# Three-pass weight tiles between the heads of an attention loop, gate writes in eighths, and four value buffers at the end of an expert sweep

## The chip, the cores and the metric

The kernel runs on one core of one Trainium2 chip. The metric is the device time of one execution in microseconds; less is better. TensorE's granted clock has two levels here, 1.2 and 2.4 GHz; a clock of 1.00 in a row is 2.4 GHz throughout the stretch.

## What is computed

One layer of a hybrid block on 512 tokens of width 1024, in float32, ending in a norm. Cut to what matters:

```python
mod = silu(c) @ w_ada + b_ada            # shift1, scale1, gate1, shift2, scale2, gate2
h = modulate(rmsnorm(x), shift1, scale1)
proj = h @ w_in                          # qa ka va | qb kb vb | ga gb
ya = swa_sink_attention(rope(qa), rope(ka), va, sinks) @ w_up_swa   # 8 heads, 2 of keys, window 128
yb = stick_breaking_attention(qb, kb, vb) @ w_up_sb                 # 8 heads, strictly causal
x = x + gate1 * ((sigmoid(ga) * ya + sigmoid(gb) * yb) @ w_out)
h2 = modulate(rmsnorm(x), shift2, scale2)
# PEER: product keys pick 16 of 16384 experts for each of 8 heads and token
x = x + gate2 * sum_k gelu(h2 . expert_u[k]) * g[k] * expert_v[k]
out = rmsnorm(x)
```

## The kernel before

The kernel is one program with an order written out by hand for each engine; semaphores join them. SP (SyncE) issues nearly all loads, in one order, and a wait on it holds up all loads behind it. An engine's buffers lie in one arena, and areas are used again from stage to stage.

**Start.** Six parts of `mod` come from twelve 2 MB tiles of `w_ada`, through a ring of four slots: VectorE multiplies a tile with `silu(c)` (`ada_product`, 8 steps) and TensorE sums over the partitions (`ada_sum`, four f32 products of one column); the third tile goes through TensorE directly. Then `h` is normed and modulated (ScalarE L839). VectorE works out the rope angles behind that (L1132 to L1142).

**Head loop** (about 53 to 439 us). Four pairs of heads. Each turn loads `w_pair` (2 MB, from GpSimd's queue) and makes the projections qa, qb, kb (L584) and vb (L588) in plain f32 from `h`. VectorE makes two ada products, then rope. For each of the two heads follow sliding-window scores (L606 to L613, the head's 64 rows), stick-breaking scores in four blocks of 512 to 128 columns in four PSUM banks (L619), one gate block of 512 tokens, in f32 (L625, kept in `early_gates`), the turned probabilities (L632), the sums of the logarithms (L638 to L643), and the two outputs of 64 columns (L649, L655). Beside it ScalarE takes absolute values, exponentials and logarithms, VectorE maxima, scalings and copies out of PSUM.

**Up and out** (439 to 581 us). `UNITS` lists 24 weight tiles of 128x1024: 8 ups, the 8 gate blocks of m = 4 to 7 between them, and 8 outs. Each is split into a high part (ScalarE `unit_high` L893) and a low part (VectorE `unit_low` L1198), two tiles deep, and TensorE makes three passes (`PASSES`: high x high, low x high, high x low) in float32r, so 24 products of 512 columns a tile (L691). The first ups use the gates that were kept. After the last up all of `merged` is split (L910, L1202; seven of the eight low parts come ahead of the last merge).

**Ranking** (594 to 873 us). Queries, top-k and the first 36 chunks (`EARLY`) of `expert_u`: `scores(c)` is 24 products of 384 columns (L729). The 384 tokens of three tiles take all experts in chunks of 128 (there are 128 chunks); the fourth tile's tokens take their 128 picked experts by gathers (`gather` L506), with VectorE's `dot` (L1243) and `add_row` (L1350).

**Gates** (873 to 1124 us). 36 chunks (`BESIDE`) of scores with 96 groups of one-hot products (L773) between them. After each 16 groups a stage buffer of 4 MB is full, and SP writes it to memory with two transfers of 2 MB in runs of 256 bytes (L429), between the loads of `expert_u` (`u_load` L406). Scores before `STASHED` are passed through gelu and put into memory too.

**Values.** Four more chunks of scores, then 52 (`NF`) steps of one `scores` and one `values(i)` (18 products of 512 columns, L785), to 1595 us, then 76 steps of `values` alone, to 1939 us. Weights are gelu x gate (VectorE `weights` L1395), split by ScalarE (L1066) and VectorE (L1400) into one of two `ar` buffers; value rows are split by ScalarE (L1051) and VectorE (L1383) into one of two `vs` buffers. Each engine does one chunk and waits for the next one. `dots_before` and `accs_before` say how many dots and added rows lie between. At the end the last chunk finishes all six banks, tile by tile, and VectorE and ScalarE do gate2, sum, norm and output of four token tiles (L1422 to L1431).

## Time and profile before

| | us |
|---|---|
| median of 3 runs (1956.57 to 1959.97) | 1956.68 |
| profiled execution | 1958.36 |
| its span, first to last instruction | 1956.4 |

| engine | busy us | share |
|---|---|---|
| TensorE products | 1815.1 | 93% |
| TensorE weight loads | 1500.4 | 77% |
| VectorE | 1325.8 | 68% |
| ScalarE | 693.5 | 35% |
| GpSimd | 535.2 | 27% |

The chain of work that ended last is TensorE for 74% of the span, VectorE 10%, DMA 5%, ScalarE 5%. TensorE's weight loads (PEld) overlap its products (PE). In the rows below, the view of windows gives for each stretch its length and, for PE, PEld, DVE (VectorE), ACT (ScalarE) and POOL (GpSimd), busy us and the number of instructions, then the granted clock, the share of the DMA engines and GB/s. In a timeline a row is a group of like instructions in a row: start, length, and in brackets the idle time before it with what ended it. An f32 product is recorded as two instructions, a three-pass one as one for each pass. L12 is line 12 of the kernel.

### The profile page before, as it was taken

What the parts mean: (1) busy time and instruction counts of PE and PEld (TensorE: products, weight loads), DVE (VectorE), ACT (ScalarE), POOL (GpSimd) and SP (SyncE); (2) the same over time, 40 slices, a digit from 0 to 9 for tenths busy, and PEclk for the clock granted to TensorE, in tenths of its full rate; (3) what the DMA queues carried; (4) which work ended last, traced back from release to release, by engine and by line L of the source; (5) the groups of instructions that cost most, each with busy time, mean ns of one, the idle gap of its engine ahead of it and who ended that gap; (6) DMA issues with size and microseconds to landing.
All of it is one profiled execution on the core that took longest, in us unless ns stands there. A gap on an engine that the chain in (4) does not pass through costs nothing.

```text
span 1956.4 us, 24506 instructions
## 1 busy us (share of the span) xinstructions
PE 1815.1 (93%) x8747; PEld 1500.4 (77%) x8747; DVE 1325.8 (68%) x2755; ACT 693.5 (35%) x1072; POOL 535.2 (27%) x326
## 2 busy tenths in 40 slices
PE   5899999989988999989989969999999999999996
PEld 4555555558867999979989959999999987777774
DVE  5423232335437699989788848888877888888886
ACT  2231415153326444334343323333333333333333
POOL 0000000000004576460000035545553443333330
PEclk7989798889998999989999989999999999999998
DMA  8414030202222434346888799999998989999992
GB/s 314 179 43 150 12 139 21 86 7 90 93 90 81 143 119 144 98 160 164 221 241 226 204 324 377 338 344 335 339 339 297 324 311 341 342 338 341 344 342 107
DMA packets 221696, 416.21 MB, mean 213 GB/s; under 512 B 112305, under 2 KB 148145, under 8 KB 217649
## 3 DMA queue, kind: packets, MB, share of 16 engines
q1 hardware_dynamic: 173232, 257.70, 39.3%
q0 software_dynamic: 37440, 142.62, 20.5%
...
## 4 chain that ended last, share of the span: by engine, by line
PE 74%; DVE 10%; DMA 5%; ACT 5%; issue 4%; SPq 2%; POOL 0%; DVEq 0%; ACTq 0%
PE bank L729 22%; PE bank L785 19%; PE bank L691 6%; PE bank L584 4%; PE bank L709 4%; DMA u_raw<-euT 4%; PE bank L625 3%; PE bank L773 2%; PE bank L619 2%; PE bank L588 1%; ACT v_split L1051 1%; DVE hot_j L1361 1%; PE bank L613 1%; DVE weights L1395 1%; DVE row_sum L1350 1%
## 5 line engine op out<-in xcount | busy, mean ns | idle before, releaser
L729 PE MATMUL bank<-h_split,u_split 128*128 128x384 f32 x3072 | 564.3, 340 | 18.3 <-DVE u_split L1339 15.7
L785 PE MATMUL bank<-v_split,a_split 128*128 128x512 f32 x2304 | 547.4, 393 | 21.8 <-DVE a_split L1400 20.0
L729 PEld LDWEIGHTS bank<-h_split,u_split 128*128 128x128 f32 x3072 | 541.0, 190 | 24.7 <-DVE u_split L1339 16.0
L785 PEld LDWEIGHTS bank<-v_split,a_split 128*128 128x128 f32 x2304 | 428.3, 188 | 127.6 <-issue 40.7
L506 POOL DMA_INDIRECT rows<-eu,idx x128 | 184.7, 1443 | 401.6 <-DVE dots L1243 376.7
L506 POOL DMA_INDIRECT rows<-ev,idx x128 | 180.4, 1410 | 269.7 <-DVE row_sum L1350 238.4
L1051 ACT ACTIVATE v_split<-v_raw 128x1024 fp32r<-128x1024 f32 x128 | 135.6, 1059 | 178.9 <-PE bank L785 174.9
L953 ACT ACTIVATE gelus<-bank 128x384 f32<-128x384 f32 x128 | 62.9, 491 | 352.7 <-PE bank L729 349.6
L1383 DVE TENSOR_TENSOR v_split<-v_raw,v_split 128x1024 fp32r<-128x1024 f32 x128 | 156.5, 1223 | 18.5 <-ACT v_split L1051 18.1
L1350 DVE SCALAR_TENSOR_TENSOR row_sum<-rows,agate,row_sum 128x1024 f32<-128x1024 f32 x127 | 162.6, 1280 | 4.3
L1339 DVE TENSOR_TENSOR u_split<-u_raw,u_split 128x1024 fp32r<-128x1024 f32 x90 | 109.9, 1221 | 74.3 <-ACT u_split L944 73.8
L944 ACT ACTIVATE u_split<-u_raw 128x1024 fp32r<-128x1024 f32 x128 | 134.5, 1052 | 56.6 <-DMA u_raw<-euT 56.6
L1243 DVE CUSTOM_DVE_ANT_0 rows<-rows,h_rows 128x1024 f32<-128x1024 f32 x128 | 150.6, 1220 | 1.7 <-issue 1.6
L1066 ACT ACTIVATE a_split<-weights 128x384 fp32r<-128x384 f32 x128 | 66.8, 522 | 173.0 <-DVE weights L1395 172.3
L483 POOL TENSOR_TENSOR query_lo<-query_raw,query_hi 128x2048 fp32r<-128x2048 f32 x8 | 37.3, 4663 | 322.0 <-ACT query_hi L937 322.0
L488 POOL TENSOR_TENSOR u_split<-u_raw,u_split 128x1024 fp32r<-128x1024 f32 x38 | 92.2, 2438 | 94.1 <-ACT u_split L944 94.1
L1395 DVE TENSOR_TENSOR weights<-gelus,gates 128x384 f32<-128x384 f32 x128 | 70.9, 554 | 57.9 <-issue 49.1
L773 PE MATMUL bank<-hot_i,hot_j 128*128 128x128 f32 x768 | 93.7, 276 | 14.3 <-ACT stage L1040 12.0
L1361 DVE TENSOR_SCALAR hot_j<-cst,slots_turned 128x128 f32<-128x128 f32 x384 | 106.3, 340 | 0.0
L1400 DVE TENSOR_TENSOR a_split<-weights,a_split 128x384 fp32r<-128x384 f32 x128 | 71.1, 555 | 51.9 <-ACT a_split L1066 51.9
L773 PEld LDWEIGHTS bank<-hot_i,hot_j 128*128 128x128 f32 x768 | 91.4, 192 | 15.6 <-issue 12.8
L709 PE MATMUL bank<-h_split,query_hi 128*128 128x512 f32 x256 | 81.9, 396 | 12.9 <-DVE h_split L1237 12.9
...
## 6 DMA issues: line engine op xcount, KB each, us to landing
u_raw<-euT SPq DMA_DIRECT2D x128, 512.0 KB
v_raw<-ev SPq DMA_DIRECT2D x128, 512.0 KB
arena<-w_ada SPq DMA_DIRECT2D x12, 2048.0 KB, 7.9
gates_scratch<-stage SPq DMA_DIRECT2D x12, 2048.0 KB, 19.6
gates<-gates_scratch SPq DMA_DIRECT2D x128, 192.0 KB
...
arena<-w_units SPq DMA_DIRECT2D x24, 512.0 KB, 3.5
```

Source lines behind the costliest of these rows:

```text
L506: pool.indirect_dma_start(rows[g % NG], None, eu if g < P else ev_rows, bass.IndirectOffsetOnAxis(ap=idx[:, g % P:g % P + 1], axis=0)).the ...
L691: last = pe.matmul(ps[bank][:], ws[:, t % 2, wp, k * P:(k + 1) * P], x_split[:, xp, k, :], start=(first and q == 0), stop=(end and q == 2))
L709: last = pe.matmul(ps[c][:], q_parts[n % 2][wp][:, k * 256 + c * P:k * 256 + (c + 1) * P], hs[:, xp, k, :], start=(k == 0 and q == 0), sto ...
L729: last = pe.matmul(ps[6 + b][:, 0:TD], us[:, b, wp, k * P:(k + 1) * P], hs[:, xp, k, 0:TD], start=(k == 0 and q == 0), stop=(k == DC - 1 a ...
L773: last = pe.matmul(ps[2 + b][:, q * P:(q + 1) * P], ohj[:, b, q, :], ohi[:, b, q, :], start=True, stop=True)
L785: last = pe.matmul(ps[2 * t + f][:], ar[:, b, ap, t * P:(t + 1) * P], vs[:, b, vp, f * 512:(f + 1) * 512], start=(first and q == 0), stop= ...
L944: act_(us[:, c % 2, 0, :], ut[:, c % RING, :], ACT.Copy).then_inc(u_hi, 1)
L1051: act_(vs[:, i % 2, 0, :], vt[:, i % RING, :], ACT.Copy).then_inc(v_hi, 1)
L1243: nv.tensor_tensor_reduce(rows[k % NG], rows[k % NG], hT, 1.0, 0.0, ALU.mult, ALU.add, dots[:, k:k + 1]).then_inc(rows_used, 1)
L1350: nv.scalar_tensor_tensor(acc, rows[g % NG], agate[:, k:k + 1], acc, ALU.mult, ALU.add).then_inc(rows_used, 1)
L1361: ins = nv.tensor_scalar(ohj[:, b, q, :], cst[:, K_IOTA:K_IOTA + P], slotsT[:, 1, t:t + 1], slotsT[:, 2, t:t + 1], ALU.is_equal, ALU.mult)
L1383: nv.tensor_tensor(vs[:, i % 2, 1, :], vt[:, i % RING, :], vs[:, i % 2, 0, :].bitcast(F32), ALU.subtract).then_inc(v_split, 1)
```

## The change

All 50 weight tiles of the attention and merge stages (18 projections, 16 gate blocks, 8 ups, 8 outs) now form one list `BLOCKS` and take one path: `block_load` on SP, four raw slots deep, `block_high` on ScalarE, `block_low` on GpSimd, two split buffers, three passes on TensorE. `h` is split into `h1s` at the start, by VectorE, chunk by chunk. Six blocks (`LEAD`) come before the first head; the others lie between the steps of the eight heads (`FILL`: two after the scores, the others after the sums), all 16 gates among them. Values are projected like the others and turned by TensorE (`turn_values`). The angles are made before the first ada product. The queries of a pair lie in two buffers padded to 128 rows with zeros (`qR`, `qB`). Stick-breaking scores take three banks instead of four, in packed buffers; the ada products go on in slot 0 alone, one a head, and each `ada_load` on SP stands before the block loads of a head. Ups and outs follow each other with no gate between them, and all low parts of `merged` come after the last merge.

Gates are written in eighths (`PIECES`), with a load of `expert_u` after each of the pieces 1 to 6. `BEFORE` sets eight chunks of scores instead of four between gates and values (with two dots each), so `STASHED` is 80 and `NF` 48; dots and rows are spread anew. In the steps of values alone there are four buffers (`v_late`, `a_late`) instead of two, ScalarE and VectorE work a chunk ahead, and the last four chunks (`LATE`) are summed token tile by token tile. The core of the diff:

```diff
-STASHED = EARLY + BESIDE + 4
+BEFORE = 8
+STASHED = EARLY + BESIDE + BEFORE
+LATE = 4
+PIECES = 8
 NF = NK - STASHED
 NG = 5
 DOTS_HEAD = 0
 DOTS_RANK = DOTS_HEAD * (HEADS - 1)
-DOTS_G = DOTS_RANK + GROUPS // 8 + 8
-DOTS_BY = 36
-ACC_FROM = 37
-ACC_F = 42
-ADA = (5, 5, 1, 1)
+DOTS_G = DOTS_RANK + GROUPS // 8 + 2 * BEFORE
+DOTS_BY = 34
+ACC_FROM = 35
+ACC_F = 38
...
-UNITS = ([("up", m, 0) for m in range(4)]
-         + [u for m in range(4, DC) for u in (("gate", m, 0), ("gate", m, 1), ("up", m, 0))]
-         + [("out", m, 0) for m in range(DC)])
+FILL = [[("gate", 0), ("gate", 1), ("v", 1), ("gate", 2)],
+        [("q", 1), ("qb", 1), ("kb", 1)],
+        [("gate", 3), ("gate", 4), ("v", 2), ("gate", 5)],
+        [("q", 2), ("qb", 2), ("kb", 2)],
+        [("gate", 6), ("gate", 7), ("v", 3), ("gate", 8)],
+        [("q", 3), ("qb", 3), ("kb", 3)],
+        [("gate", 9), ("gate", 10), ("gate", 11), ("gate", 12)],
+        [("gate", 13), ("gate", 14), ("gate", 15)]]
+LEAD = [("k", 0), ("v", -1), ("q", 0), ("qb", 0), ("kb", 0), ("v", 0)]
+BLOCKS = LEAD + [b for f in FILL for b in f] + [("up", m) for m in range(DC)] + [("out", m) for m in range(DC)]
+AT = {b: t for t, b in enumerate(BLOCKS)}
+UNIT0 = AT[("up", 0)]
+
+
+def block_banks():
+
+    banks = [5 + t % 2 for t in range(len(LEAD))]
+    other = {}
+    for n, fill in enumerate(FILL):
+        first = banks[-1] if n else 5
+        for k in range(len(fill)):
+            banks.append(first if k % 2 == 0 else 11 - first)
+        other[n] = 11 - banks[-1]
+    return banks, other
+
+
+BANK, OB_BANK = block_banks()
+SB_AT = ((0, 0), (1, 0), (2, 0), (1, 384))
+SB_PACK = (0, 512, 896, 1152, 1280)
+SB_ORDER = (0, 2, 1, 3)
...
+            def block_load(t):
+
+                if t >= 4:
+                    sp.wait_ge(w_split, t - 3)
+                sp.dma_start(wraw[:, t % 4, :], w_blocks[t]).then_inc(w_in[t % 4], 16)
+
+            def ada_load(n):
+
+                sp.wait_ge(ring_free[0], n - 3 + FREE)
+                sp.dma_start(ring[:, 0, :], w_ada[n]).then_inc(ring_in[0], 16)
+
+            for t in range(4):
+                block_load(t)
+            ada_load(4)
+            for t in range(4, len(LEAD) + 4):
+                block_load(t)
+            for n in range(HEADS):
+                if n + 5 < 12:
+                    ada_load(n + 5)
+                for k in range(len(FILL[n])):
+                    block_load(AT[FILL[n][k]] + 4)
+            for t in range(UNIT0 + 4, len(BLOCKS)):
+                if t == UNIT0 + 8:
+                    sp.wait_ge(sig_ready, 8)
+                    for s in range(2):
+                        sp.dma_start(q_raw[s], w_qry[s]).then_inc(q_in[s], 16)
+                block_load(t)
...
             for n in range(GROUPS // 16):
-                for k in range(6):
-                    u_load(EARLY + RING + 6 * n + k)
+                if n == 0:
+                    for k in range(6):
+                        u_load(EARLY + RING + k)
                 for b in range(4):
                     sp.wait_ge(staged[b], 4 * (n + 1) + FREE)
-                for i0 in range(0, NK, NK // 2):
-                    sp.dma_start(gates_dram[i0:i0 + NK // 2, :, n * 64:n * 64 + 64].rearrange("i j t -> j i t"),
-                                 stages[n % 2][:, i0:i0 + NK // 2, :]).then_inc(g_out[n % 2], 16)
-            for c in range(EARLY + BESIDE + RING, STASHED + RING):
+                for k in range(PIECES):
+                    i0 = k * NK // PIECES
+                    sp.dma_start(gates_dram[i0:i0 + NK // PIECES, :, n * 64:n * 64 + 64].rearrange("i j t -> j i t"),
+                                 stages[n % 2][:, i0:i0 + NK // PIECES, :]).then_inc(g_out[n % 2], 16)
+                    if 1 <= k <= 6:
+                        u_load(EARLY + RING + 6 * (n + 1) + k - 1)
+            for c in range(EARLY + RING + BESIDE + 6, STASHED + RING):
                 u_load(c)
...
+            nc.gpsimd.memset(qR, 0.0)
+            nc.gpsimd.memset(qB, 0.0).then_inc(padded, 1)
+
+            def block_low(t):
+
+                pool.wait_ge(w_hi, t + 1)
+                nc.gpsimd.tensor_tensor(ws[:, t % 2, 1, :], wraw[:, t % 4, :], ws[:, t % 2, 0, :].bitcast(F32), ALU.subtract).then_inc(w_split, 1)
+
+            for t in range(len(BLOCKS)):
+                block_low(t)
...
+            def block(t, bank):
+
+                pe.wait_ge(w_split, t + 1)
+                before = [s for s in range(max(0, t - 4), t) if BANK[s] == bank]
+                if before:
+                    evacuated(pe, before[-1])
                 for k in range(DC):
-                    last = pe.matmul(ps[1][:, t * P:(t + 1) * P], h[:, k, t * P:(t + 1) * P], kavaw[:, k, P:2 * P],
-                                     start=(k == 0), stop=(k == DC - 1))
-            last.then_inc(va_done, 1)
+                    if t == 0:
+                        pe.wait_ge(h1_split, k + 1)
+                    for q, (wp, xp) in enumerate(PASSES):
+                        last = pe.matmul(ps[bank][:], ws[:, t % 2, wp, k * P:(k + 1) * P], h1s[xp][:, k, :],
+                                         start=(k == 0 and q == 0), stop=(k == DC - 1 and q == 2))
+                last.then_inc(block_done, 1)
...
+            block(0, BANK[0])
+            block(1, BANK[1])
             pe.wait_ge(q_raw_ready, 1)
...
+            pe.matmul(ps[7][:], cst[:, K_ROT:K_ROT + P], qraw, start=True, stop=True).then_inc(rot_done, 1)
+            block(2, BANK[2])
+            turn_values(-1)
+            block(3, BANK[3])
+            rotate(0)
+            block(4, BANK[4])
+            block(5, BANK[5])
+            pe.wait_ge(v_ready, 1)
+            turn_values(0)
+            for n in range(HEADS):
+                i, a = n // 2, n % 2
+                heads_scores(n)
+                for k, b in enumerate(FILL[n]):
+                    if k == 1 and n:
+                        pe.wait_ge(ob_out, n)
+                    if k == 2:
+                        if b[0] == "kb":
+                            pe.wait_ge(oa_out, n)
+                            rotate(i + 1)
+                        turn_probs(n)
+                        later_sums(n)
+                    block(AT[b], BANK[AT[b]])
+                head_outputs(n)
+                if a == 0 and i + 1 < PAIRS:
+                    turn_values(i + 1)
...
-            def values(i, b, first=False, final=False):
+            def values(i, a, v, tiles=range(ND), first=False, final=False):
 
                 pe.wait_ge(v_split, i + 1)
                 pe.wait_ge(a_split, i + 1)
-                for t in range(ND):
+                for t in tiles:
                     for f in range(2):
                         for q, (ap, vp) in enumerate(PASSES):
-                            last = pe.matmul(ps[2 * t + f][:], ar[:, b, ap, t * P:(t + 1) * P], vs[:, b, vp, f * 512:(f + 1) * 512],
+                            last = pe.matmul(ps[2 * t + f][:], a[:, ap, t * P:(t + 1) * P], v[:, vp, f * 512:(f + 1) * 512],
                                              start=(first and q == 0), stop=True, skip_group_check=True)
-                    if final:
-                        last.then_inc(bank_final, 1)
-                if not final:
+                if final:
+                    last.then_inc(bank_final, 1)
+                elif tiles == range(ND):
                     last.then_inc(v_done, 1)
...
                 last.then_inc(g2_done, 1)
-            with pe.Fori(NF // 2, NK // 2 - 1) as r:
-                for e in range(2):
-                    values(r * 2 + e, e)
-            values(NK - 2, 0)
-            values(NK - 1, 1, final=True)
+            with pe.Fori(NF // LATE, NK // LATE - 1) as r:
+                for e in range(LATE):
+                    values(r * LATE + e, a_late[:, e], v_late[:, e])
+            for t in range(ND):
+                for e in range(LATE):
+                    values(NK - LATE + e, a_late[:, e], v_late[:, e], tiles=[t], final=(e == LATE - 1))
...
+            def block_high(t):
+
+                sa.wait_ge(w_in[t % 4], 16 * (t // 4 + 1))
+                if t >= 2:
+                    sa.wait_ge(block_done, t - 1)
+                act_(ws[:, t % 2, 0, :], wraw[:, t % 4, :], ACT.Copy).then_inc(w_hi, 1)
...
+            for n in range(HEADS):
+                i, a = n // 2, n % 2
+                t0 = AT[FILL[n][0]]
+                for k, b in enumerate(SB_ORDER):
+                    bank, col = SB_AT[b]
+                    sa.wait_ge(sb_scored, 4 * n + SB_WHOLE[k])
+                    act_(spl[b], ps[bank][:, col:col + T - b * P], ACT.Abs).then_inc(abs_ready, 1)
+                for k, b in enumerate(SB_ORDER):
+                    sa.wait_ge(abs_ready, 4 * n + k + 1)
+                    act_(spl[b], spl[b], ACT.Exp, scale=-1.0).then_inc(act_steps, 1)
+                sa.wait_ge(max_ready, n + 1)
+                for t in range(TT):
+                    act_(prob[:, t, :], ps[3 + t // 2][:, (t % 2) * 256:(t % 2) * 256 + 256], ACT.Exp,
+                         bias=mx[:, 4 + t:5 + t], accum_out=sk4[:, t:t + 1]).then_inc(swa_exp, 1)
+                act_(sk4[:, 4:8], mx[:, 4:8], ACT.Exp, bias=sml[:, S_SINK + n:S_SINK + n + 1]).then_inc(swa_exp, 1)
+                for k, b in enumerate(SB_ORDER):
+                    sa.wait_ge(act_steps, 4 * n + k + 1)
+                    act_(spl[b], spl[b], ACT.Ln, bias=1.0).then_inc(log_ready, 1)
+                evacuate(t0)
+                block_high(t0 + 2)
+                evacuate(t0 + 1)
+                block_high(t0 + 3)
+                sa.wait_ge(probT_done, n + 1)
+                for c in range(2):
+                    last = act_(probT[:, 2 * c:2 * c + 2, :].rearrange("p a b -> p (a b)"), ps[3 + c][:], ACT.Copy)
+                last.then_inc(probT_ready, 1)
+                for k, b in enumerate(SB_ORDER):
+                    bank, col = SB_AT[b]
+                    sa.wait_ge(sb_summed, 4 * n + SB_WHOLE[k])
+                    if n:
+                        sa.wait_ge(ob_done, n)
+                    act_(atB[b], ps[bank][:, col:col + T - b * P], ACT.Exp).then_inc(at_ready, 1)
+                for k in range(2, len(FILL[n])):
+                    evacuate(t0 + k)
+                    block_high(t0 + k + 2)
+                if a == 0 and i + 1 < PAIRS:
+                    value_rows(i + 1)
...
+            for k in range(DC):
+                ve.wait_ge(h_ready, k + 1)
+                nv.tensor_copy(h1s[0][:, k, :], h[:, k, :]).then_inc(h1_hi, 1)
+                ve.wait_ge(h1_hi, k + 1)
+                nv.tensor_tensor(h1s[1][:, k, :], h[:, k, :], h1s[0][:, k, :].bitcast(F32), ALU.subtract).then_inc(h1_split, 1)
...
+            weights(NF)
+            a_low(NF)
+            for i in range(NF, NK):
                 if i + 1 < NK:
+                    weights(i + 1)
                     v_low(i + 1)
+                    a_low(i + 1)
+                for k in range(accs_before(i), accs_before(i + 1)):
+                    add_row(k)
```

## Rows read from the trace of the kernel before

**Rows 1.** Windows by stage, whole core; columns as told above
```profile
106.00:439.50 333.50, 314.97 (x1119) 184.56 (x1119) 105.23 (x223) 112.75 (x256) 1.06 (x2) 0.85 0.17 64
439.50:581.00 141.50, 140.20 (x591) 112.36 (x592) 61.38 (x77) 48.49 (x67) 0.00 (x0) 0.98 0.29 96
873.40:1124.30 250.90, 236.64 (x1609) 235.26 (x1609) 206.62 (x527) 99.58 (x167) 12.62 (x11) 0.99 0.77 211
1124.30:1170.20 45.90, 27.47 (x148) 26.86 (x146) 19.84 (x28) 10.97 (x17) 13.38 (x9) 0.81 1.02 317
1590.00:1939.40 349.40, 330.24 (x1409) 258.41 (x1407) 278.41 (x320) 122.11 (x157) 120.80 (x84) 1.00 0.90 319
1939.40:1956.40 17.00, 0.00 (x0) 0.00 (x0) 12.88 (x17) 4.92 (x11) 0.00 (x0) 0.60 0.31 123
```

**Rows 2.** Timeline of TensorE, 135 to 181 us: start, length, operation, [idle before]
```profile
135.70 0.30 PE L606 MATMUL bank<-never_r,ident_r 128*128 128x128 f32 x1 [0.98 <-DVE arena L1188]
...
139.18 2.32 PE L619 MATMUL bank<-arena 64*128 64x512 f32 x8
141.42 7.13 PE L625 MATMUL bank<-h,arena 128*128 128x512 f32 x16
...
149.94 1.12 PE L638 MATMUL bank<-arena,cst 128*128 128x512 f32 x2 [0.51 <-DVE arena L1181]
...
154.86 1.74 PE L649 MATMUL bank<-arena 128*64 128x128 f32 x14
...
160.08 20.84 PE L584 MATMUL bank<-h,arena 128*128 128x512 f32 x48 [1.32 <-issue]
```

**Rows 3.** Timeline of TensorE, 188 to 204 us
```profile
188.46 1.94 PE L546 MATMUL bank<-cst,arena 128*128 128x1 f32 x16 [0.40 <-PE bank L588]
...
199.20 4.47 PE L619 MATMUL bank<-arena 64*128 64x512 f32 x8
```

**Rows 4.** Timeline of VectorE, 0 to 25 us
```profile
17.55 0.49 DVE L1103 TENSOR_SCALAR arena<-arena,cact 128x512 f32<-128x512 f32 x1 [17.55 <-DMA arena<-w_ada]
```

**Rows 5.** Timeline of ScalarE, 40 to 60 us
```profile
47.43 5.75 ACT L839 ACTIVATE h<-h,mod,mul 128x512 f32<-128x512 f32 x8 [22.73 <-DVE mul L1129]
```

**Rows 6.** View by line: shortest/median/longest ns, first to last start (us)
```profile
L893 ACT ACTIVATE unit_split<-arena x24: 1044/1060/1062, 431.4 to 566.6; 128x1024 fp32r<-128x1024 f32 x24
...
L488 POOL TENSOR_TENSOR u_split<-u_raw,u_split x38: 2342/2393/3372, 607.1 to 863.7; 128x1024 fp32r<-128x1024 f32 x38
...
L1233 DVE TENSOR_TENSOR h<-x,rstd x8: 677/678/3500, 586.0 to 593.0; 128x512 f32<-128x512 f32 x8
```

**Rows 7.** Timeline of TensorE, 541 to 554 and 1582 to 1606 us
```profile
541.48 6.04 PE L691 MATMUL bank<-h_split,unit_split 128*128 128x512 f32 x24
...
547.82 6.04 PE L691 MATMUL bank<-h_split,unit_split 128*128 128x512 f32 x24
...
1582.97 4.35 PE L729 MATMUL bank<-h_split,u_split 128*128 128x384 f32 x24
1587.16 8.36 PE L785 MATMUL bank<-v_split,a_split 128*128 128x512 f32 x36
1595.36 1.95 PE L807 MATMUL bank<-cst,mod 128*128 128x128 f32 x16
1597.06 8.44 PE L785 MATMUL bank<-v_split,a_split 128*128 128x512 f32 x36
```

**Rows 8.** DMA issues: out<-in, queue, count, KB each, median us to landing
```profile
arena<-w_ada SPq DMA_DIRECT2D x12, 2048.0 KB, 7.9
gates_scratch<-stage SPq DMA_DIRECT2D x12, 2048.0 KB, 19.6
...
arena<-w_units SPq DMA_DIRECT2D x24, 512.0 KB, 3.5
```

**Rows 9.** Waits, 1124.3 to 1170.2 us: waiting <- releaser, us, times, longest
```profile
PE bank L729 <- DVE u_split L1339: 15.7, 1, 15.7
```

**Rows 10.** Groups of instructions, 1590 to 1940 us: busy, mean ns, idle before
```profile
L1400 DVE TENSOR_TENSOR a_split<-weights,a_split 128x384 fp32r<-128x384 f32 x76 | 42.4, 558 | 50.6 <-ACT a_split L1066 50.6
```

673 lines of the change are left out of this document (332 added, 341 removed).

## The prediction

> **What bounds the kernel now.** I read the windows by stage first, because one share for the whole span mixes stages with different limits. In [rows 1] TensorE is busy for 314.97 of the 333.50 us of the head loop, for 140.20 of 141.50 in the up and out stage, for 236.64 of 250.90 while the gates are built, but only for 27.47 of 45.90 in the gap before the values and 330.24 of 349.40 in the last values. So the first two stages are bound by TensorE's work and by its clock; to shorten them its work has to shrink. The granted clock in the same rows is 0.85 in the head loop and 0.98 to 1.00 in the others but the gap: the loop loses 0.15 x 333.5 = 50 us to half speed. Two rows show it: the stick-breaking score products of one head take 2.24 us (139.18 to 141.42, [rows 2]) and in another 4.47 [rows 3]. In the gap the longest wait is for the subtraction of an expert chunk, 15.7 us, once [rows 9], behind gate writes on the queue. In the last values no load is waited for: VectorE stands idle for 50.6 us, 76 times 0.66, for ScalarE's copy of the weights [rows 10]; with 278.41 us of work in 349.4 that makes it the engine that sets the pace, 4.5 us a chunk (1597.06 to 1939.4 for 76, [rows 7]).
>
> **Part by part, against the span of 1956.4 us.** 1.96 us lie around it (profiled execution 1958.36); the median of the three runs, 1956.68, is 1.7 us below that.
>
> *Price of a projection block.* An f32 block of 512 tokens costs 20.84 / 3 = 6.95 us at full clock [rows 2]. Three passes are 24 products of 512 columns; 36 of them take 1595.36 - 1587.16 = 8.20 us [rows 7], so a block is 24 x 8.20 / 36 = 5.47 us. 18 projection blocks and the 8 early gate blocks get cheaper; the 8 late gate blocks cost what they did and move into the head loop.
>
> *Up to the first head.* Before, its scores start at 106.0. The steps that make the angles move ahead of VectorE's first load, for which it waited until 17.55 [rows 4]; I count 0.7 us of lateness for them (ends 0 and 2). ScalarE now copies two weight blocks ahead of the modulation, which started at 47.43 [rows 5]. They can be loaded only into a ring slot that is freed at about 46, and a block of that size lands after 3.5 us [rows 8]: with two copies of 1.06 [rows 6] and a gap the modulation starts at 52.3, 5 us later. Then VectorE makes 8 pairs of copy and subtraction, about 1.25 us each, which pace the first block; it ends at 65.5. Five more blocks make 27.4, rotations, turns and waits 4: first head at 97, **-9 us**.
>
> *Head loop.* A head without its gate block, at full clock [rows 2]: sliding-window scores 139.18 - 135.70 = 3.48; stick scores 2.24; turned probabilities 149.94 - 0.51 - (141.42 + 7.13) = 0.88; sums 154.86 - 149.94 = 4.92; outputs (160.08 - 1.32) - 154.86 = 3.90; together 15.42, eight times 123.4. The queries padded with zeros to 128 rows are shown nowhere; I price them as the 64-row ones, since the number of columns stays (the ends are the same price, and a gain in clock, below). Added: 28 blocks x 5.47 = 153.2; seven ada sums at 1.94 / 2 = 6.8 [rows 3]; three rotations and three turned value blocks, estimated as 4.8. Sum 288.2. Waits: the sums could start 10.76 us after the sliding scores' end (149.94 - 139.18), 0.51 of it a wait; now two blocks and the turned probabilities, 11.8 us, stand between. So it is covered with 1 us to spare; I keep 8 us, 1 a head (ends 0 and 28). Clock: I keep 5 of the 50 us (ends 0 and 46), because half speed came behind one-column products and idle time (188.46 on, [rows 3]) and in 64-row scores, and the new order puts full blocks on both sides and pads the rows. Entry to the up stage 5.5. End: 97 + 288.2 + 8 + 5 + 5.5 = 403.7 against 439.5; the stretch behind the first head is 306.7 against 333.5: **-26.8 us**.
>
> Who else works in that loop: a block's chain is load, ScalarE copy 1.06, GpSimd subtraction 2.39 [rows 6], TensorE; it may take 5.47 and takes 3.6. VectorE's product of two SBUF operands takes 0.68 us and once 3.50 [rows 6], where GpSimd was subtracting. Four subtractions a head can shift VectorE by up to 2.4 us each, mostly under the two blocks; this is why 8 us stay for waits. The Trainium skill ("SBUF — State Buffer", "Who interferes with whom") says that a VectorE instruction with two SBUF inputs and a GpSimd instruction that reads SBUF hold each other off for the whole instruction, which speaks against this change; the trace agrees in that one row. By that rule taken at its worst, once for each of 28 blocks, the sum would be up to 28 x 2.4 = 67 us higher. SP is one queue: its ada load waits for VectorE's product (about 23 us into a head), and the head's block loads stand behind it; 2 MB land after 7.9 us and a block after 3.5 [rows 8]: 23 + 7.9 + 3.5 + 3.5 = 38 us, wanted at about 42. Hidden with 4 us of slack.
>
> *Up and out.* 8 ups x 5.47 = 43.8 and 2.5 cold at the entry as before; outs at 6.34 (541.48 to 547.82, [rows 7]) and their end as now, 45.3; the low parts of merged now all follow the last merge, 3.5 us of wait, and one GpSimd collision 1.5. 96.6 against 141.5: **-44.9 us**.
>
> *Gates in eighths.* A whole write lands after 19.6 us [rows 8] and SP has the expert loads behind it; now a load follows each piece. TensorE's own work is 236.64 [rows 1]; I take 240: **-10.9 us**, ends -14 and -4.
>
> *Gap, fused stage, last values.* The gap now holds 10 chunk scores instead of 6: 4.19 each (1582.97 to 1587.16, [rows 7]) make 41.9. In it must be moved the last gates (4.2 MB), 8 expert chunks (4.2), 11 to 16 gathers of 0.5 MB, 4 value chunks, gates and stashes: 18 to 22 MB, at the 317 GB/s of the gap's row 57 to 69 us. I take 57.4, since loads now slip in between the pieces (ends 43 and 66): **+11.5 us**. The fused stage loses four steps of 4.19 + 4.10: **-33.2**. Last values, 80 chunks: TensorE alone 4.10; VectorE 278.41 / 76 = 3.66 once its wait is gone; transfers 1.54 MB a chunk, 4.35 at the 354 GB/s that 319 at a share of 0.90 means [rows 1]. I take 4.3: 344 against 342.3, **+1.7**, ends -14 (4.10) and +18 (4.50).
>
> *End.* Of 17.0 us behind the last product VectorE works 12.88 [rows 1]. With the last four chunks by token tile two thirds of that can lie beside 10.9 us of products; but four chunks must be ready within 4 us rather than 16. **-7 us**, ends -10 and 0.
>
> Sum: -9 - 26.8 - 44.9 - 10.9 + 11.5 - 33.2 + 1.7 - 7 = -118.6; 1958.4 - 118.6 = **1840 us**.
>
> **Rivals.**
> (a) *The clock falls in every head all the same.* For: the loop keeps 64-column outputs and one-column sums, and half speed came back in every pair. Against: before, it needed idle time or half-filled rows. Price: 0.15 x 307 = 46 instead of 5: 1881.
> (b) *ScalarE, GpSimd and VectorE can't keep two blocks ahead.* For: ScalarE runs in order, had 112.75 / 8 = 14 us of work a head [rows 1] and gets 4 x 1.06 more; the 3.50 us row. Price: one subtraction and one copy exposed in each head instead of 1 us, 8 x 3.45 - 8 = 20: 1860 (at the rule's worst 1900).
> (c) *The new buffers of the last values do nothing, since transfers set the pace.* It stays 4.5 a chunk, +16, and the end wins nothing, +7: 1863.
> (d) *Slower than before.* The one mechanism large enough is SP's queue in the head loop, where the blocks stand behind 2 MB. It decides from 4 us of slack + 119 / 8 = 19 us beyond what I counted, a landing of some 22 us instead of 3.5; the gates' writes show 19.6. At 26 us each head waits 18 us: 1840 - 8 + 8 x 18 = 1976. Against: the landings of weights in [rows 8].
> That the change doesn't do what it says can only be in part here: (c).
>
> **Chances.** Forecast 0.47, (a) 0.18, (b) 0.18, (c) 0.15, (d) 0.02. The range goes from 1802 (lower ends of the head loop, the gap, the last values and the end: -13, -14, -8 of 16, -3) to 1884, which takes in (a). A difference below 0.2%, 4 us, can't be told from none here. Faster by more than that 0.97, within it 0.01, slower 0.02.
>
> **What would show it.** Right: first head near 97, up stage near 404, a clock of 0.95 or more between them, gates built in about 240 us, last values at 4.3 us a chunk with no wait of VectorE for ScalarE's copy, some 10 us behind the last product. Wrong: a clock of 0.85 in the loop (a); TensorE released by GpSimd's subtraction (b); ScalarE released by v_raw, or VectorE by the gates, in the last stage (c); ScalarE's block copy released by a load (d). The sum itself is most open in the gap, whose price lies between -3 and +20.

## The result and the profile after

| | before | after |
|---|---|---|
| median of 4 runs | 1958.33 us | 1791.37 us (1790.34 to 1792.58) |
| after / before | | 0.9148, 95% interval 0.9132 to 0.9163 |
| span of the profiled execution | 1956.4 us | 1788.5 us |

The change takes 167 us off, where 118.6 were forecast: 1791.4 lies below the range of 1802 to 1884. The direction was right, the size was not.

Windows of the kernel after, cut at the same events as [rows 1]: the head loop, the up and out blocks, the gates, the gap, the last 80 value chunks (in the kernel before their like begins at 1597.0, 7 us into its row) and the end. Columns: stretch, length, busy time (instructions) of TensorE, its weight loads, VectorE, ScalarE and GpSimd, granted clock, DMA share, GB/s.

```profile
94.80:371.60 276.80, 275.46 (x1356) 217.33 (x1355) 156.94 (x251) 137.53 (x284) 69.39 (x29) 1.00 0.29 110
371.60:470.00 98.40, 95.59 (x398) 75.51 (x398) 47.84 (x47) 36.75 (x54) 34.18 (x14) 0.98 0.31 108
762.60:994.70 232.10, 232.10 (x1614) 232.10 (x1613) 208.29 (x526) 101.03 (x168) 12.56 (x11) 1.00 0.85 227
994.70:1058.50 63.80, 44.41 (x238) 43.27 (x236) 33.18 (x48) 16.17 (x24) 23.12 (x17) 0.88 1.04 353
1453.20:1779.70 326.50, 326.50 (x1443) 270.17 (x1441) 287.27 (x339) 124.58 (x169) 110.78 (x85) 1.00 0.94 355
1779.70:1788.50 8.80, 0.18 (x1) 0.00 (x0) 5.32 (x7) 1.45 (x3) 0.00 (x0) 0.77 0.45 179
```

What to see against [rows 1]: the head loop holds 8 more blocks (three passes each) and is 56.7 us shorter; its clock went from 0.85 to 1.00, and TensorE is idle in it for 1.3 us, all of it at the entry to the ups. While the gates are built and in the last values TensorE is busy in every microsecond. Only in the gap is it not, and there the DMA share is 1.04. The end fell from 17.0 to 8.8 us.

Timeline of TensorE in the kernel after, the first head's scores, which answers [rows 2]:

```profile
94.80 2.32 PE L674 MATMUL bank<-arena 128*128 128x512 f32 x8
96.88 0.30 PE L683 MATMUL bank<-never_r,ident_r 128*128 128x128 f32 x1
...
97.52 0.59 PE L688 MATMUL bank<-arena 128*128 128x256 f32 x2
...
98.87 0.82 PE L648 MATMUL bank<-h_hi_part,block_split 128*128 128x512 f32 x2
```

The sliding-window scores take 98.87 - 96.88 = 1.99 us where [rows 2] had 3.48 at the same full clock. A pair of 256-column products takes 0.59 us with queries padded to 128 rows.

Waits in the kernel after: waiting <- releaser, us, times, longest. The first line is TensorE's in the gap, for the first weights ([rows 9] had 15.7 us for an expert chunk), the second ScalarE's in the head loop, the last two are from the last values, where [rows 10] had VectorE waiting 50.6 us for ScalarE's copy.

```profile
PE bank L887 <- DVE a_split L1555: 12.3, 1, 12.3
```
```profile
ACT block_split L949 <- DMA arena<-w_blocks: 35.6, 11, 10.0
```
```profile
ACT v_late L1191 <- PE bank L887: 164.4, 69, 2.6
DVE v_late L1538 <- ACT v_late L1191: 30.7, 41, 1.9
```

ScalarE does wait for weight blocks in the head loop, 11 times, but TensorE has two blocks in hand and never waits. In the last values ScalarE now waits for TensorE, as it should; VectorE still waits 30.7 us for ScalarE, for value rows and no longer for weights, but TensorE has no gap there.

The miss by stage (us, each against the same stretch of before, the fused stage there up to 1597.0; the sum is the whole difference of the spans):

| stage | forecast | measured | difference |
|---|---|---|---|
| up to the first head | -9 | -11.2 | -2.2 |
| head loop | -26.8 | -56.7 | -29.9 |
| up, out, norm, ranking | -44.9 | -42.9 | +2.0 |
| gates in eighths | -10.9 | -18.8 | -7.9 |
| gap | +11.5 | +17.9 | +6.4 |
| fused stage | -33.2 | -32.1 | +1.1 |
| last values | +1.7 | -15.9 | -17.6 |
| end | -7 | -8.2 | -1.2 |
| sum | -118.6 | -167.9 | -49.3 |

Three terms carry it: the head loop, the last values and the gates.

### The profile page after: what moved, and what is told of

Its sections match the earlier page's. It is cut to its first block, busy times and chain, and to the rows that moved or that the text cites. A ratio compares the mean times of both kernels' runs of the same rounds, so it can differ in the third digit from the quotient of the medians.

```text
span 1788.5 us, 24191 instructions
## 1 busy us (share of the span) xinstructions
PE 1703.4 (95%) x8735; PEld 1497.3 (84%) x8735; DVE 1359.3 (76%) x2755; ACT 710.7 (40%) x1096; POOL 643.1 (36%) x374
## 4 chain that ended last, share of the span: by engine, by line
PE 91%; DMA 3%; DVE 3%; ACT 1%; POOL 1%; issue 0%; SPq 0%; DVEq 0%; ACTq 0%
PE bank L887 29%; PE bank L831 28%; PE bank L648 11%; PE bank L793 5%; PE bank L875 5%; PE bank L811 5%; DMA u_raw<-euT 1%; PE bank L708 1%; PE bank L674 1%; PE bank L710 1%; PE bank L732 1%; PE bank L821 1%; PE bank L615 1%; PE bank L724 1%; DMA gates_scratch<-stage 1%; DMA gates<-gates_scratch 1%
## 5 line engine op out<-in xcount | busy, mean ns | idle before, releaser
L887 PE MATMUL bank<-v_late,a_late 128*128 128x512 f32 x1440 | 326.7, 389 | 0.0
L887 PEld LDWEIGHTS bank<-v_late,a_late 128*128 128x128 f32 x1440 | 270.2, 188 | 56.1
L535 POOL TENSOR_TENSOR block_split<-arena,block_split 128x1024 fp32r<-128x1024 f32 x50 | 121.2, 2427 | 336.4 <-ACT block_split L949 336.4
L887 PE MATMUL bank<-v_split,a_split 128*128 128x512 f32 x864 | 208.1, 395 | 12.3 <-DVE a_split L1555 12.3
L887 PEld LDWEIGHTS bank<-v_split,a_split 128*128 128x128 f32 x864 | 163.4, 190 | 45.3 <-issue 12.6
L648 PE MATMUL bank<-h_hi_part,block_split 128*128 128x512 f32 x544 | 172.8, 399 | 8.7 <-DVE h_lo_part L1297 8.7
L1191 ACT ACTIVATE v_late<-v_raw 128x1024 fp32r<-128x1024 f32 x80 | 84.8, 1060 | 166.2 <-PE bank L887 164.4
L648 PEld LDWEIGHTS bank<-h_hi_part,block_split 128*128 128x128 f32 x544 | 102.5, 190 | 30.9 <-issue 9.7
L1538 DVE TENSOR_TENSOR v_late<-v_raw,v_late 128x1024 fp32r<-128x1024 f32 x80 | 97.9, 1223 | 32.9 <-ACT v_late L1191 30.7
L648 PE MATMUL bank<-h_lo_part,block_split 128*128 128x512 f32 x272 | 106.9, 393 | 0.0
```

The costliest lines, as they stand in the source:

```text
L535: nc.gpsimd.tensor_tensor(ws[:, t % 2, 1, :], wraw[:, t % 4, :], ws[:, t % 2, 0, :].bitcast(F32), ALU.subtract).then_inc(w_split, 1)
L648: last = pe.matmul(ps[bank][:], ws[:, t % 2, wp, k * P:(k + 1) * P], h1s[xp][:, k, :], start=(k == 0 and q == 0), stop=(k == DC - 1 and q ...
L887: last = pe.matmul(ps[2 * t + f][:], a[:, ap, t * P:(t + 1) * P], v[:, vp, f * 512:(f + 1) * 512], start=(first and q == 0), stop=True, sk ...
L1538: nv.tensor_tensor(v_buffer(i)[:, 1, :], vt[:, i % RING, :], v_buffer(i)[:, 0, :].bitcast(F32), ALU.subtract).then_inc(v_split, 1)
```

## Experiments

**1. The changed kernel with 64-row scores.**

```diff
-pe.matmul(ps[bank][...], kB[:, b * P:(b + 1) * P], qB[:, a, b * P:T], ...)
+pe.matmul(ps[bank][...], kB[lo:hi, b * P:(b + 1) * P], qB[lo:hi, a, b * P:T], ...)
...
-last = pe.matmul(at, qR[:, a, t * P:(t + 1) * P], kR[:, (t - 1) * P:(t + 1) * P], ...)
+last = pe.matmul(at, qR[lo:hi, a, t * P:(t + 1) * P], kR[lo:hi, (t - 1) * P:(t + 1) * P], ...)
```

> The changed kernel, but each head's two kinds of scores read only the head's own 64 rows of queries and keys (the padded buffers are still there, the zero half is not used). Theory A (the full 128 rows are what made the scores cheap): the sliding-window scores go from about 2.0 us a head back to about 3.5 and the stick scores from 2.1 to 2.2, so the head loop is 8 x 1.6 = 13 us longer and the kernel takes about 1804; the granted clock of the loop stays above 0.97. Theory B (they became cheap because the clock is full and nothing waits): within 3 us of the changed kernel, 1791. Theory C (half-filled rows are what lets the clock fall): the loop's clock falls to 0.85 or so and the kernel takes 1830 or more.

1815.4 us: 24 more than the changed kernel. Its head loop, and TensorE's timeline across the scores of two heads:

```profile
95.10:395.30 300.20, 298.86 (x1355) 224.39 (x1353) 155.97 (x251) 137.64 (x283) 71.05 (x29) 0.97 0.27 102
```
```profile
136.80 0.33 PE L684 MATMUL bank<-never_r,ident_r 128*128 128x128 f32 x1
...
137.58 0.38 PE L688 MATMUL bank<-window_r,ident_r 128*128 128x256 f32 x1
137.90 0.70 PE L689 MATMUL bank<-arena 64*128 64x256 f32 x2
138.52 0.38 PE L688 MATMUL bank<-window_r,ident_r 128*128 128x256 f32 x1
...
140.40 0.73 PE L648 MATMUL bank<-h_hi_part,block_split 128*128 128x512 f32 x2
...
171.68 0.70 PE L689 MATMUL bank<-arena 64*128 64x256 f32 x2
...
172.62 1.13 PE L689 MATMUL bank<-arena 64*128 64x256 f32 x2
...
174.19 1.22 PE L689 MATMUL bank<-arena 64*128 64x256 f32 x2
175.34 1.22 PE L648 MATMUL bank<-h_hi_part,block_split 128*128 128x512 f32 x2
...
180.15 0.62 PE L648 MATMUL bank<-h_hi_part,block_split 128*128 128x512 f32 x2
```

The loop is 23.4 us longer. In one head the scores take 3.60 us at full clock (136.80 to 140.40), 1.6 more than 1.99: 13 us for eight, Theory A. The stick scores add some 1.5: 2.35 us a head from start to start against 2.08 to 2.18. In the next head the products nearly double their length in the middle of the scores, with no idle time before them, and stay slow for some 7 us, into the block behind; in four of the eight heads the clock falls there or at the scores' end. The other 9 us are this: 0.03 of clock on 300 us. Theory C is right in kind, A in the larger part; neither alone gives 24.

Why the 64-row form costs more stands in the weight loads. Timeline of TensorE's loads, first here, then in the changed kernel:

```profile
137.58 0.19 PEld L688 LDWEIGHTS bank<-window_r,ident_r 128*128 128x128 f32 x1
137.90 0.29 PEld L689 LDWEIGHTS bank<-arena 64*128 64x128 f32 x2
138.52 0.19 PEld L688 LDWEIGHTS bank<-window_r,ident_r 128*128 128x128 f32 x1 [0.33 <-issue]
```
```profile
97.32 0.36 PE L687 MATMUL bank<-window_r,ident_r 128*128 128x256 f32 x1
97.41 0.31 PEld L688 LDWEIGHTS bank<-arena 128*128 128x128 f32 x2
97.74 0.19 PEld L687 LDWEIGHTS bank<-window_r,ident_r 128*128 128x128 f32 x1
```

Here the loads start at 137.58, 137.90 and 138.52, the moments at which their own products start: nothing is loaded ahead where 128-row masks and 64-row queries take turns. From 136.80 to 140.40 this happens eight times, and a load takes 0.19 us, so I estimate that it makes 1.5 of the 1.6 us. In the changed kernel the queries' load starts at 97.41, inside the mask's product (97.32 to 97.68), and the next mask's at 97.74, before its product at 97.77. The stick scores, which do not alternate, cost nearly the same in both forms (2.42 us against 2.32 to 2.42), so it is the alternation, not the 64 rows as such. The Trainium skill ("TensorE: Matmul & The Clock Gate", "Step-by-step: what each phase is for") says that a load is pulled ahead of running products when the row groups don't conflict or when it goes to the background weight buffer. In these rows it is pulled ahead only where the row count stays the same from one product to the next. The same section says that the time of a load does not depend on its row count; the trace agrees (0.19 us with 64 rows at 134.98 and with 128 at 137.58).

**2. The kernel before with padded queries only.**

```diff
-        qR = carve(T)
-        qB = carve(T)
+        qR = carve(2, T)
+        qB = carve(2, T)
...
+            nc.gpsimd.memset(qR, 0.0)
+            nc.gpsimd.memset(qB, 0.0).then_inc(padded, 1)
...
-last = pe.matmul(at, qR[lo:hi, t * P:(t + 1) * P], kR[lo:hi, (t - 1) * P:(t + 1) * P], ...)
+last = pe.matmul(at, qR[:, a, t * P:(t + 1) * P], kR[:, (t - 1) * P:(t + 1) * P], ...)
```

(the same in the stick scores, and in the copies and rotations that write the two halves)

> The kernel before with one thing of the change: two zero-padded query buffers a pair, and scores over all 128 rows. Theory A: the head loop is 10 to 13 us shorter (8 heads x 1.3 to 1.6) and its clock stays at 0.85, so about 1946. Theory C (the 64-row scores let the clock fall): the loop's clock rises towards 1.00 and it gets 30 to 50 us shorter, 1910 to 1928. Theory B: nothing, 1957; the two smaller rotations on VectorE cost at most 1 us a pair.

1922.5 us, 0.9813 of before (0.9795 to 0.9832): 37 us from the padding alone. Its head loop, then the gate block's line in the head loop of the kernel before and of this one: busy us, mean ns.

```profile
105.40:402.40 297.00, 272.27 (x1118) 170.47 (x1118) 108.59 (x229) 113.26 (x259) 1.05 (x2) 0.95 0.19 71
```
```profile
L625 PE MATMUL bank<-h,arena 128*128 128x512 f32 x128 | 72.1, 727 | 0.0
```
```profile
L629 PE MATMUL bank<-h,arena 128*128 128x512 f32 x128 | 56.3, 592 | 0.0
```

The loop goes from 333.5 to 297.0 and its clock from 0.85 to 0.95. The gate block behind the scores (L625, L629) has 128 rows in both kernels, yet gives 15.8 us back: in the kernel before part of it ran at half speed behind 64-row scores. TensorE's busy time falls by 42.7 us (314.97 to 272.27), more than the loop, since its waits grow from 18.5 to 24.7. With run 1's 1.6 us a head the padding is worth some 13 us by itself, and the other 30 of the 42.7 come through the clock; the waits take 6 back. Theory C, with A's price in it.

**3. The kernel before with the new last stage only** (as in the change: the buffers, the weights one chunk ahead, the last four chunks by token tile).

```diff
+        def v_buffer(i):
+            return vs[:, i % 2] if i < NF else v_late[:, i % LATE]
...
-            with pe.Fori(NF // 2, NK // 2 - 1) as r:
-                for e in range(2):
-                    values(r * 2 + e, e)
+            with pe.Fori(NF // LATE, NK // LATE - 1) as r:
+                for e in range(LATE):
+                    values(r * LATE + e, a_late[:, e], v_late[:, e])
```

> The kernel before with the change's last stage alone: four value buffers, weights one chunk ahead, the last four chunks by token tile; its last stage has 76 chunks. Theory A (VectorE's wait for ScalarE's copy set 4.5 us a chunk, and behind it comes TensorE's own work): 4.08 us a chunk, 310 instead of 342 us, and the end 8 us shorter, so 1918. Theory B (as I forecast, a transfer ceiling of 354 GB/s holds it at 4.35): 331 us, and 1938 with the end. Theory C (the late stage is fast only because the changed kernel enters it with its loads ahead): 4.5 us a chunk, 1950.

1916.4 us, 0.9789 (0.9764 to 0.9813). The windows of its last 76 chunks and of its end:

```profile
1591.70:1902.10 310.40, 310.40 (x1375) 257.16 (x1374) 274.31 (x325) 118.97 (x161) 107.55 (x81) 1.00 0.94 355
```
```profile
1902.10:1911.40 9.30, 0.68 (x3) 0.21 (x2) 5.64 (x8) 1.85 (x6) 0.00 (x0) 0.80 0.42 169
```

310.4 / 76 = 4.08 us a chunk, TensorE without a gap, the end 9.3 us. Theory A: it had 4.08 and 310 us, and the stage owes nothing to the rest of the change, where a chunk takes 326.5 / 80 = 4.08 too. The stage starts 5 us earlier than in the kernel before (1591.7 against 1597.0), which is within what executions of that kernel differ by (1957 to 1964). At 355 GB/s the chunk moved 1.45 MB, which a ceiling of 354 would let through in 4.1 us: this run refutes the 1.54 MB of the forecast, not yet the ceiling.

**4. The changed kernel without the weave.**

```diff
                 heads_scores(n)
+                turn_probs(n)
+                later_sums(n)
                 for k, b in enumerate(FILL[n]):
                     ...
                     if k == 2:
                         ...
-                        turn_probs(n)
-                        later_sums(n)
```

> The changed kernel with the weave undone on TensorE: in each head the turned probabilities and the stick sums stand right behind the scores, and all blocks of the head behind them. Theory A (the two blocks between are what hides the softmax chain; in the changed kernel the stick terms are ready 10.9 us after the scores end): TensorE waits about 10 us in each head, 80 us in all, and the kernel takes 1870; if the clock falls after the idle time, up to 46 us more, 1915. Theory B (the three-pass blocks alone made the gain, the order is worth little): under 1805.

1882.0 us, 91 more. Its head loop, and what TensorE waited for in it:

```profile
95.00:463.40 368.40, 312.68 (x1358) 239.20 (x1355) 143.47 (x251) 135.65 (x284) 74.73 (x29) 0.87 0.23 83
```
```profile
PE bank L696 <- DVE arena L1339: 43.1, 8, 5.4
PE bank L605 <- DVE arena L1348: 7.2, 7, 1.0
```
```profile
104.88 1.97 PE L696 MATMUL bank<-cst,arena 128*128 128x128 f32 x8 [5.38 <-DVE arena L1339]
```

TensorE is idle for 368.4 - 312.7 = 55.7 us and busy for 37.2 us more with the same work, at a clock of 0.87: the turned probabilities behind a wait take 1.97 us instead of 1.03 in the first head of the changed kernel. So Theory A, though with shorter waits (some 6.4 us a head instead of 10) and most of the clock's price: 54 of the 92 us that the weave saves in this loop are waits, 37 are slow products behind them. Without it the loop, with its 8 extra blocks, would be longer than before.

**5. The changed kernel with whole writes of the gates.**

```diff
-PIECES = 8
+PIECES = 2
...
-                if n == 0:
-                    for k in range(6):
-                        u_load(EARLY + RING + k)
+                for k in range(6):
+                    u_load(EARLY + RING + 6 * n + k)
...
-                    if 1 <= k <= 6:
-                        u_load(EARLY + RING + 6 * (n + 1) + k - 1)
```

> The changed kernel with each group of gates written in two halves and six expert loads ahead of them, as before; all else is the change's. Theory A (a load behind each eighth is what keeps the loads coming): ScalarE waits for u_raw again (39.6 us before, 0 in the changed kernel while the gates are built), TensorE for the stages (12.0 us before), and the gates take 240 to 251 us instead of 232: 1799 to 1810. Theory B (the gates got faster only since ScalarE, TensorE and the loads enter the stage in another order): within 3 us of 1791.

1817.2 us, 26 more. The gates and the gap, and the waits while the gates are built:

```profile
763.40:1016.60 253.20, 239.61 (x1611) 238.47 (x1610) 207.42 (x530) 99.78 (x167) 12.65 (x12) 0.97 0.78 211
1016.60:1085.20 68.60, 43.95 (x241) 43.31 (x239) 33.77 (x48) 16.43 (x24) 24.19 (x17) 0.84 1.00 326
```
```profile
ACT u_split L1079 <- DMA u_raw<-euT: 40.4, 5, 8.8
...
PE bank L872 <- ACT stage L1175: 12.8, 5, 3.3
```

The gates take 253.2 instead of 232.1 us and the gap 4.8 more. Of the 21 us 13.6 are waits of TensorE and 7.5 are slower products, at a clock of 0.97. The eighths are worth 26 us, beyond both my forecast and Theory A's upper end.

**6. The changed kernel with two of three products in the last 80 chunks** (the product of the weights' high part and the values' low part is left out there).

```diff
-values(r * LATE + e, a_late[:, e], v_late[:, e])
+values(r * LATE + e, a_late[:, e], v_late[:, e], passes=PASSES[:2])
```

> The changed kernel without the third product (high part of the weights by low part of the values) in the last 80 chunks, so that TensorE needs 2.72 us a chunk instead of 4.08 and what stands behind it shows. A chunk moves 355 GB/s x 4.08 us = 1.45 MB and costs VectorE 287.27 / 80 = 3.59 us. Theory A (my forecast's ceiling of 354 GB/s): 4.08 us a chunk as now, 1791. Theory B (the transfers can go at 400 GB/s): 3.6 to 3.7 us a chunk, VectorE nearly always busy, 1757 to 1763. Theory C (ceiling at 377, the rate of most slices): 3.85 us, 1773.

1775.6 us, the median of two runs. The last 80 chunks, and the waits in them:

```profile
1454.00:1762.80 308.80, 245.52 (x963) 178.90 (x961) 281.57 (x336) 123.56 (x164) 126.25 (x85) 0.97 0.98 375
```
```profile
PE bank L887 <- DVE a_late L1555: 63.2, 73, 3.5
```
```profile
ACT v_late L1191 <- DMA v_raw<-ev: 19.9, 22, 1.4
```

3.86 us a chunk at 375 GB/s: Theory C's number. Whether the transfers (0.98) or VectorE (281.6 of 308.8 us) end it the run does not tell apart; either way my ceiling of 354 GB/s was none, and both lie below TensorE's 4.08.

**7. Four instead of sixteen dots in the gap.**

```diff
-                for k in range(2):
-                    dot(DOTS_G - 2 * (STASHED - c) + k)
+                if (STASHED - c) % 2 == 0:
+                    dot(DOTS_G - (STASHED - c) // 2)
```

> The changed kernel with 4 instead of 16 gathered rows' dot products in the gap between the gates and the values; the other 12 follow in the fused stage, at 3.3 instead of 2.9 a step. Theory A (the gap is as long as its transfers, 22.5 MB at 353 GB/s): 12 gathers of 0.5 MB less are 6.3 MB, 18 us; the gap takes 46 to 50 us instead of 63.8, and the fused stage at 8.22 us a step has room for them within 3 us: 1775 to 1780. Theory B (the gap is the chain from the last gate write over the gate loads to the first weights, which waits 12.3 us in its last part): at most 5 us, 1787. Theory C (the dots come back in the fused stage, whose transfers already take 0.92): no change, 1791.

1777.5 us, 14 less than the changed kernel. The gap and the fused stage:

```profile
995.90:1047.30 51.40, 41.65 (x238) 40.73 (x237) 19.48 (x24) 16.11 (x23) 4.67 (x5) 0.96 1.04 320
1047.30:1440.80 393.50, 393.48 (x1983) 357.50 (x1984) 334.87 (x454) 137.12 (x190) 218.81 (x150) 1.00 0.95 346
```

12.4 us out of the gap, and the fused stage, which takes the 12 gathers over, is not longer (394.7 in the changed kernel). Theory A, at two thirds of its price: 6.3 MB less, but 353 GB/s became 320, and the share stayed at 1.04: what is left moves more slowly, probably the gates' small writes, which no run separates. In the changed kernel the first 25 us of the gap go at 321 GB/s and the rest at 374.

**8. The modulation in front, and the first low parts on VectorE.** First the order alone, then with the first two blocks' low parts moved from GpSimd to VectorE.

```diff
-            block_high(0)
-            block_high(1)
             sa.wait_ge(mod_ready, 1)
-            modulate(0, mul1, 0)
+            modulate(0, mul1, 0, range(3))
+            block_high(0)
+            modulate(0, mul1, 0, range(3, 6))
+            block_high(1)
+            modulate(0, mul1, 0, range(6, DC))
```

The second edit, on GpSimd and on VectorE:

```diff
-            for t in range(len(BLOCKS)):
+            pool.wait_ge(w_split, 2)
+            for t in range(2, len(BLOCKS)):
                 block_low(t)
...
+                if k in (1, 3):
+                    t = k // 2
+                    ve.wait_ge(w_hi, t + 1)
+                    nv.tensor_tensor(ws[:, t, 1, :], wraw[:, t, :], ws[:, t, 0, :].bitcast(F32), ALU.subtract).then_inc(w_split, 1)
```

> The changed kernel with ScalarE's modulation in front: three parts, the first block's copy, three parts, the second copy, two parts. Theory A (the modulation, which waits 3.8 us for two copies of blocks that land at 49, delays the first block): VectorE's pairs start at 48.5 instead of 52.2, the first block at about 53.2 instead of 55.8 and the kernel is 2 to 4 us shorter, 1788. Theory B (the first block's own weights set its start, or its subtraction on GpSimd collides with VectorE's pairs for longer): no change or up to 2 us longer.

1789.5 us against 1791.4: too little to tell from none by the times. In the timelines of the changed kernel, of this one, and of the next the first block starts at:

```profile
55.76 1.19 PE L648 MATMUL bank<-h_hi_part,block_split 128*128 128x512 f32 x2 [8.65 <-DVE h_lo_part L1297]
```
```profile
51.05 2.72 DVE L1299 TENSOR_TENSOR h_lo_part<-h,h_hi_part 128x512 fp32r<-128x512 f32 x1
...
53.47 1.19 PE L648 MATMUL bank<-h_hi_part,block_split 128*128 128x512 f32 x2 [6.38 <-POOL block_split L535]
```
```profile
52.23 1.19 PE L649 MATMUL bank<-h_hi_part,block_split 128*128 128x512 f32 x2 [5.13 <-DVE block_split L1304]
```

> The changed kernel with the modulation in front as in the run before, and the first two blocks' low parts on VectorE (1.22 us each) instead of GpSimd (2.4 each). Theory A (VectorE and GpSimd hold each other off: two of VectorE's subtractions took 2.72 and 2.74 instead of 0.69 us while GpSimd worked, 4.1 us for two): all eight take 0.69, the first block's weights are there at 52.0 instead of 53.3 and the first head's scores start at about 92.5 (94.8 in the changed kernel): 1788. Theory B (VectorE's own 2.4 us more cost as much as the collisions): first head at 94 to 95, 1791.

1787.6 us. The line of the eight low parts (shortest/median/longest ns) in the changed kernel and in this one:

```profile
L1297 DVE TENSOR_TENSOR h_lo_part<-h,h_hi_part x8: 691/693/2720, 52.9 to 62.4; 128x512 fp32r<-128x512 f32 x8
```
```profile
L1300 DVE TENSOR_TENSOR h_lo_part<-h,h_hi_part x8: 691/692/694, 48.9 to 58.8; 128x512 fp32r<-128x512 f32 x8
```

With GpSimd idle none takes 2.72 us. So the collision of which the forecast spoke under the Trainium skill's "SBUF — State Buffer", "Who interferes with whom", is real, and cost 2.0 us here. In the head loop of the changed kernel, where GpSimd subtracts in every head, some of VectorE's ada products and of its masks of the stick terms are slower too (same view):

```profile
L1256 DVE SCALAR_TENSOR_TENSOR arena<-arena,cact x77: 750/752/2915, 18.2 to 360.7; 128x512 f32<-128x512 f32 x77
L1348 DVE TENSOR_TENSOR arena<-arena,cst x32: 280/289/2485, 106.7 to 352.7; 128x128 f32<-128x128 f32 x32
```

In the head loop they take 1044 and 631 ns on average (56 and 32 of them), and in that of the kernel before 752 and 286. That is some 27 us of VectorE's time in these two lines, and none of it reached TensorE. The first block starts 3.5 us earlier, as Theory A has it, and the first head's scores too (91.25); but at the start of the ranking 2.2 us of it are left (482.3 against 484.5), and at its end 0.3 (762.28 against 762.57). What takes it back was not tested.

**9. The gap's queue in another order, and all together.** The first of three kernels is run 7's with the queue in another order, the second has both edits of run 8 besides, and the third no dots in the gap at all.

```diff
-                    if 1 <= k <= 6:
+                    if n + 1 < GROUPS // 16 and 1 <= k <= 6:
                         u_load(EARLY + RING + 6 * (n + 1) + k - 1)
+                    if n + 1 == GROUPS // 16 and k % 2:
+                        u_load(EARLY + RING + 6 * (n + 1) + k // 2)
...
-            for i in range(RING):
-                v_load(i)
+            v_load(0)
             sp.wait_ge(g_out[1], 16 * PIECES * GROUPS // 32)
             for i in range(RING):
                 gate_load(i)
+            for i in range(1, RING):
+                if i < 3:
+                    u_load(STASHED + 1 + i)
+                v_load(i)
```

> The kernel with 4 dots in the gap, and its queue in another order: in the last group of gates an expert load follows each second eighth (four instead of six), then two more, one value chunk, the gate chunks as soon as the last write has landed, and the last two expert chunks and three value chunks behind them. Theory A (in the last part of the gap TensorE waits 8.9 us for the chain last write, gate load, weights; its last write is issued only when VectorE has freed six expert buffers, and the gate loads stand behind 2 MB of values): the last write is issued some 10 us earlier and the gate loads are short, the gap takes 43 to 46 instead of 51.4 us: 1770. Theory B (the gap is as long as its transfers, whatever their order; the share is 1.04): 50 to 52 us, 1777, since an earlier write only delays a load.

> Both of these in one kernel. If the gains add, it is as much faster than the kernel with 4 dots in the gap as the two are together: 1767 by Theory A of both, 1777 by Theory B of both.

> The same with no dots in the gap, so that 116 instead of 112 follow in 34 fused steps. Theory A (the gap is bound by transfers): another 2 MB less, 4 us, and the fused stage stays at 8.2 us a step: 1763. Theory B (TensorE's 41.7 us in the gap or the fused stage's transfers, 0.95 busy, are the bound by then): within 2 us of the kernel with 4 dots.

1773.8, 1771.0 and 1767.6 us. The gap of the first (four dots) and of the last (none):

```profile
995.60:1043.40 47.80, 41.80 (x238) 40.84 (x238) 20.15 (x24) 15.54 (x22) 4.68 (x5) 1.00 1.03 317
```
```profile
992.20:1039.40 47.20, 43.34 (x237) 42.39 (x237) 15.53 (x16) 15.49 (x22) 0.94 (x1) 0.96 1.00 297
1039.40:1431.40 392.00, 392.00 (x1985) 356.35 (x1985) 338.41 (x462) 138.02 (x190) 224.22 (x154) 1.00 0.96 353
```

The order takes 3.6 us out of the gap, half of Theory A's 7: TensorE's wait of 8.9 us for the first weights is gone, but 6.0 us of waits for expert chunks come in its place, with the transfers' share at 1.03. The second kernel lies between its Theory A (1767) and B (1777): the medians are 2.8 us apart, but in the profiled execution its gap starts 2.1 us earlier and takes 49.7 us, 1.9 more, so most of what the front gave is lost there. The third is 3.4 us faster than the second, near Theory A's 4: its gap is 2.5 us shorter and its fused stage no longer (392.0 against 392.3). The last kernel is 0.9026 of before (0.9009 to 0.9043), 1.3% faster than the changed one (0.9148), and beats both. In its gap TensorE works 43.3 of 47.2 us, and in the fused stage behind it without a break.

## Why the prediction was right in direction and wrong in size

*Head loop, missed by 29.9 us.* Three steps failed. (1) "I price them as the 64-row ones, since the number of columns stays (the ends are the same price, ...)": the padded sliding-window scores cost 1.99 us a head instead of 3.48, 12 us for eight. I had no row for such products and gave the unknown price no range at all. The column count was the wrong measure: in the 64-row form the weight loads stand between the products (run 1). (2) "Clock: I keep 5 of the 50 us": the clock is 1.00, so those 5 were too many. My reason named three causes side by side. The one-column products are still there at a clock of 1.00, so they alone do not lower it; runs 1, 2 and 4 separate the other two: 64-row scores lower the clock without idle time (9 us in the woven loop; in the kernel before, which has waits too, padding gave back some 30), and idle time lowers it without them (0.87 in run 4). The change removes both. (3) "I keep 8 us, 1 a head" of waits; TensorE has none in the heads. Together 25 us; the other 5 are in small terms, of which the entry to the up stage (2.4 us from the last one-column sum at 369.21 to 371.61, against 5.5) is the largest. Where I had a row the price held: a block was put at 5.47 us, and two take 11.12 from 98.87 to 109.99.

*Last values, missed by 17.6 us.* The wait of VectorE for ScalarE's copy did set the pace, and it went (run 3). What failed is "transfers 1.54 MB a chunk, 4.35 at the 354 GB/s", and in it the 1.54 MB: the windows give 355 x 4.08 = 1.45 MB a chunk, and [rows 1] already gave 319 x 4.5 = 1.44. With that even 354 GB/s makes 4.1 us, no more than TensorE's 4.10, my lower end, which was the answer. The 354 was no ceiling either, since a stretch at 375 GB/s exists (run 6): a rate divided by its busy share is none. It did no harm here by itself.

*Gates, missed by 7.9 us.* "TensorE's own work is 236.64 [rows 1]; I take 240": the 236.64 us held products at a lowered clock (0.99), which the waits had caused (in run 5 the waits come back, and 7.5 us of slower work with them); without waits the stage is 232.1 us, all work. Run 5 puts the eighths at 21 us in this stage and 5 in the gap.

*Gap, missed by 6.4 us the other way.* The mechanism was right: 22.5 MB were moved, against my 18 to 22, at 353 GB/s; that is within the ends of 43 to 66, but I took 57.4 from "since loads now slip in between", and the order does not shorten what the transfers bound (run 7: bytes, 12 us; run 9: order, 4 us).

*First head, up and out, fused stage, end* came within 2.2 us each. The modulation waited for the two copies until 51.3, where 52.3 was worked out.

*Rivals.* (a) the clock: it rose to 1.00. (b) two blocks ahead: ScalarE waits 35.6 us for blocks and GpSimd costs VectorE some 27 us in the loop (run 8), yet TensorE has no wait; the rule taken at its worst, 67 us, did not come. (c) fell with run 3. (d) its sign is there, ScalarE's copy released by a load 11 times, but not its price: the loop gained 56.7 us.

*The range* failed because the three largest misses all point down. The prices of the scores, the clock and the gates came from rows of the kernel before that contained the fault which the change removes (loads between products, half speed, waits); the last values had a wrong number of bytes. I widened for mishaps (1884) and gave the unpriced padding no gain.
